# Feature panels of 256 columns with high and low activations in one matmul, in a hybrid decoder layer

## What is computed

```python
proj = x @ w_in[l]                       # 2048 x 13824: q | k | v | rx | ry | gate logits
y_attn = sliding_window_attention(q, k, v, attn_sinks[l]) @ w_attn_proj[l]   # 32 heads of 64, 4 kv heads
rx = causal_dwconv(rx, rnn_conv_w[l], rnn_conv_b[l])                         # 4 taps, 2560 channels
hr = rg_lru(rx, lru_wa[l], lru_ba[l], lru_wi[l], lru_bi[l], lru_lambda[l])
y_rnn = (hr * jax.nn.gelu(ry, approximate=True)) @ w_rnn_proj[l]
g_attn, g_rnn = jnp.split(jax.nn.sigmoid(gl + b_gate[l]), 2, axis=-1)
mix = (g_attn * y_attn + g_rnn * y_rnn) @ w_out[l]
x = layer_norm(ALPHA * x + mix, ln1_g[l], ln1_b[l])
up = x @ ffn_w_up[l]
gate = causal_dwconv(x @ ffn_w_gate[l], ffn_conv_w[l], ffn_conv_b[l])        # 3 taps, 6144 channels
f = (jax.nn.gelu(gate, approximate=True) * up) @ ffn_w_down[l]
x = layer_norm(ALPHA * x + f, ln2_g[l], ln2_b[l])
```

## Time and profile before

| | |
|---|---|
| median of three runs | 1757.09 us |
| the profiled execution | 1758.42 us |
| its span, first to last instruction | 1756.6 us |
| mean granted TensorE clock | 0.991 |
| TensorE, weight loads, VectorE, ScalarE, GpSimd busy | 1717.6, 1636.3, 1033.9, 844.4, 51.1 us |
| moved by DMA | 317.14 MB, mean 181 GB/s |

### The profile page before, as it was taken

One profiled execution on the slowest core, in us unless ns is written; L12 is line 12 of the kernel. 1 busy time (PEld: TensorE's weight loads), 2 busy tenths in 40 slices (PEclk: granted clock), 3 DMA queues, 4 the chain that ended last, 5 costly groups with the idle time before them and its releaser, 6 DMA issues.

```text
span 1756.6 us, 32091 instructions
## 1 busy us (share of the span) xinstructions
PE 1717.6 (98%) x13020; PEld 1636.3 (93%) x13020; DVE 1033.9 (59%) x1182; ACT 844.4 (48%) x1027; POOL 51.1 (3%) x34
## 2 busy tenths in 40 slices
PE   7999999999999999999998999999999999999996
PEld 7999999999999999999877999999889999999885
DVE  5696695444455656556558555556454565656556
ACT  5567566444446656644335444444333444444332
POOL 0000000000000000000003000000000000000002
PEclk9999999999999999999998999999999999999998
DMA  8464453566544343456744555566555555555551
GB/s 295 141 209 158 150 198 128 193 215 199 185 149 168 119 169 131 156 192 218 261 144 144 183 179 187 191 218 200 192 191 186 186 191 190 179 182 190 192 192 72
DMA packets 157141, 317.14 MB, mean 181 GB/s; under 512 B 6008, under 2 KB 11800, under 8 KB 156312
## 3 DMA queue, kind: packets, MB, share of 16 engines
q1 hardware_dynamic: 157080, 316.28, 54.3%
HBM read 314.16 MB, written 2.10 MB: 180 GB/s over the span
## 4 chain that ended last, share of the span: by engine, by line
PE 94%; DVE 4%; ACT 1%; issue 1%; DMA 0%; DVEq 0%; SPq 0%; ACTq 0%
PE bank L268 69%; PE bank L295 20%; PE bank L491 2%; DVE w_lo L246 1%; PE bank L561 1%; PE bank L548 1%; PE bank L280 1%; DVE act_t L1162 1%; ACT s_buf L794 1%; PE bank L539 0%; DVE s_buf L1035 0%; DVE res L1223 0%; DMA x_tok<-in_x_dram 0%; DVE res L1219 0%; DVE smax L1039 0%
## 5 line engine op out<-in xcount | busy, mean ns | idle before, releaser
L268 PE MATMUL bank<-act_t,w_hi 128*128 128x256 f32 x5952 | 1065.6, 281 | 16.0 <-DVE act_t L1162 10.9
L246 DVE TENSOR_TENSOR w_lo<-raw,w_hi 128x1024 fp32r<-128x1024 f32 (+1 forms) x552 | 703.5, 1287 | 619.8 <-ACT w_hi L239 619.7
L239 ACT ACTIVATE w_hi<-raw 128x1024 fp32r<-128x1024 f32 (+1 forms) x552 | 600.2, 1095 | 763.7 <-PE bank L268 559.0
L268 PEld LDWEIGHTS bank<-act_t,w_hi 128*128 128x128 f32 x5952 | 914.3, 189 | 20.8 <-issue 16.6
L268 PE MATMUL bank<-act_t,w_lo 128*128 128x256 f32 x2976 | 834.5, 280 | 0.0
L268 PEld LDWEIGHTS bank<-act_t,w_lo 128*128 128x128 f32 x2976 | 561.3, 189 | 0.0
L295 PE MATMUL bank<-w_hi,f_t 128*128 128x512 f32 x768 | 238.6, 392 | 0.0
L295 PEld LDWEIGHTS bank<-w_hi,f_t 128*128 128x128 f32 x768 | 144.2, 188 | 32.0
L295 PE MATMUL bank<-w_lo,f_t 128*128 128x512 f32 x384 | 150.2, 391 | 0.0
L268 PE MATMUL bank<-g_t,w_hi 128*128 128x256 f32 x640 | 108.9, 276 | 0.0
L268 PEld LDWEIGHTS bank<-g_t,w_hi 128*128 128x128 f32 x640 | 96.6, 188 | 0.0
(11 more groups left out here) (137 smaller groups left out, 960.3 us busy)
## 6 DMA issues: line engine op xcount, KB each, us to landing
raw<-in_w_in_dram SPq DMA_DIRECT2D x52, 1024.0 KB, 5.1
raw<-in_ffn_w_gate_dram SPq DMA_DIRECT2D x48, 1024.0 KB, 5.1
raw<-in_ffn_w_up_dram SPq DMA_DIRECT2D x48, 1024.0 KB, 5.1
raw<-in_ffn_w_down_dram SPq DMA_DIRECT2D x48, 1024.0 KB, 5.1
raw<-in_w_in_dram SPq DMA_DIRECT2D x32, 1280.0 KB, 5.9
raw<-in_w_rnn_proj_dram SPq DMA_DIRECT2D x16, 1280.0 KB, 6.1
raw<-in_w_attn_proj_dram SPq DMA_DIRECT2D x16, 1024.0 KB, 5.2
raw<-in_w_out_dram SPq DMA_DIRECT2D x16, 1024.0 KB, 5.1
```

What stands on the lines that cost most here:

```text
L239: nc.scalar.activation(w_hi[:, slot, 0:size], raw[:, chunk, half:half + size], ACT.Copy)\
L246: nc.vector.tensor_tensor(w_lo[:, slot, 0:size], raw[:, chunk, half:half + size], w_hi[:, slot, 0:size].bitcast(F32), ALU.subtract).then_i ...
L268: last = nc.tensor.matmul(dst, w[:, slot, at_ % size:at_ % size + P], moving[:, kt, part, :], start=(kt == 0 and n == 0 and c % 2 == 0), s ...
```

## The change

- A feature panel has 256 weight columns (two tiles). The accumulator of a tile is a whole bank: w_hi streams high and low activations of a tile of features as one 512 column matmul, w_lo streams the high part, 256 columns, into the first half. The second half is added on the way out: ScalarE copies the first half out of PSUM (`first_half`), VectorE adds the second (`second_half`), and what used to read PSUM (taps, gelu, sigmoid, products) reads the SBUF copy.
- In the recurrence a group has panels of 2, 2 and 1 tiles for rx and the same for ry, 20 units of 1024 columns instead of 16 of 1280. The ry gelu and the product of a group go to the beginning of the next group.
- Chunks have 8 (10) row tiles of 256 columns, in rows of 1 KB, instead of 4 (5) of 512 in rows of 2 KB; the lone tile's chunks have rows of 512 B.
- Recurrence and attention are unrolled; feed-forward loops 12 times per half instead of 6. The attention reads q, k and v where they lie; GpSimd's staging copies go. `s_buf` goes to the ends of `raw`'s slots, the distance table and the transposed probabilities elsewhere.
- After the first LayerNorm, VectorE makes both parts of `act_t`; the affine on `res` goes from GpSimd to VectorE, a piece of 256 columns in each of the first eight turns of `ff0`. TensorE waits for all eight `ln_made` before `ff0`.
- Offsets: `act_t` 82112, `BIG` 118976, `f_t` and `ln_t` +33088, `lru_w_lo` +61760, `lru_w_hi` +75072.

The core of the diff:

```diff
-        act_t = at("act_t", 81920 + 64, [P, KT, 2, T], F32R)
+        act_t = at("act_t", 82112, [P, KT, 2, T], F32R)
-        BIG = SMALL + 3648 + 64
+        BIG = 118976
-        f_t = at("f_t", BIG + 32768, [P, FT_HALF, 2, T], F32R)
+        f_t = at("f_t", BIG + 33088, [P, FT_HALF, 2, T], F32R)
...
-        PASSES = ((w_hi, 0), (w_hi, 1), (w_lo, 0))
+        def panel_features(pe, unit, j0, acc, moving, ks, tiles, units, between=lambda j: None, kt_ready=None):
+            for j in range(units):
+                slot = (j0 + j) % 4
+                pe.wait_ge(lo_made, unit + (j0 + j + 1))
...
+                    nc.tensor.matmul(acc[:, c, :], w_hi[:, slot, at_:at_ + P], moving[:, kt, :, :].rearrange("p h t -> p (h t)"),
+                                     start=(kt == 0), stop=(kt == units * ks - 1), skip_group_check=True)
+                    last = nc.tensor.matmul(acc[:, c, 0:T], w_lo[:, slot, at_:at_ + P], moving[:, kt, 0, :],
+                                            start=False, stop=(kt == units * ks - 1), skip_group_check=True)
...
+            def first_half(name, n, used, dst, tiles=2):
+                wait_apart(unit_used, used)
+                nc.scalar.activation(dst, acc_of(name, n)[:, 0:tiles, 0:T], ACT.Copy).then_inc(half_out, 1)
...
+            def second_half(name, n, dst, tiles=2):
+                dve.wait_ge(half_out, HALVES[name] + n + 1)
+                nc.vector.tensor_tensor(dst, acc_of(name, n)[:, 0:tiles, T:2 * T], dst, ALU.add).then_inc(acc_free, 1)
```

The recurrence on ScalarE, behind the gates of a group (`fill(a, b)` splits units a to b - 1, counted from the group's start):

```diff
+                fill(19, 20)
+                gates(4)
+                fill(20, 21)
+                wait_apart(gates_read, GRP * g + GRP)
+                for c in range(GRP):
+                    nc.scalar.activation(lru_a[:, c, :], lru_r[:, c, :], ACT.Exp, ...
...
+                fill(21, 22)
+                first_half("rxy", panel + 4, unit + 18, g_work[:, GRP * g + 2:GRP * g + 4, 1, :])
+                wait_apart(v_made, g + 1)
+                nc.scalar.activation(group(0), group(0), ACT.Sqrt, scale=2.0 ** 64).then_inc(root_made, 1)
+                fill(22, 24)
```

A block of attention on ScalarE, from its eighth unit on, and the same place on VectorE:

```diff
+                refill(unit, range(11, 12), SLIM)
+                first_half(name, 2 * q + 1, unit + 8, gate[:, 2:4, :])
+                take_o(1)
+                wait_apart(acc_free, PANELS[name] + 2 * q + 4)
+                for c in range(4):
+                    done = nc.scalar.activation(gate[:, c, :], gate[:, c, :], ACT.Sigmoid, bias=param(col + 4 * q + c))
+                done.then_inc(sig_made, 1)
...
+                refill(unit, range(11, 12), SLIM)
+                second_half(name, 2 * q + 1, gate[:, 2:4, :])
+                take_o(1)
+                if name == "gr":
+                    dve.wait_ge(sig_made, q + 1)
+                    part = merge[:, 4 * q:4 * q + 4, :]
+                    nc.vector.tensor_tensor(part, part, gate, ALU.mult).then_inc(merged, 1)
```

A turn of feed-forward on VectorE:

```diff
+                refill(unit, range(6, 8), SLIM)
+                dve.wait_ge(half_out, i * 2 + (HALVES[name] + 1))
+                nc.vector.tensor_tensor(gate_raw[:, :, :], acc_of(name, 0)[:, :, T:2 * T], gate_raw[:, :, :], ALU.add)\
+                    .then_inc(acc_free, 1)
...
+                if affine:
+                    cols = ds(i * 256, 256)
+                    part = res[:, :, cols]
+                    dve.wait_ge(ln_loaded, 32)
+                    dve.wait_ge(ln_turned, 8)
+                    nc.vector.tensor_tensor(part, part, ln_gb[:, 0:1, cols].broadcast_to([P, TOK, 256]), ALU.mult).then_inc(res_made, 1)
```

More of the change, by code:

```diff
@@ L284, in panel_features, with panel_values @@
                 last.then_inc(unit_used, 1)
                 between(j)
+        def panel_values(pe, unit, j0, acc):
+            for j in range(4):
+                slot = (j0 + j) % 4
+                pe.wait_ge(lo_made, unit + (j0 + j + 1))
+                for t in range(TOK):
+                    for k in range(4):
+                        kt = 4 * j + k
+                        for n, (w, part) in enumerate(((w_hi, 0), (w_lo, 0), (w_hi, 1))):
+                            last = nc.tensor.matmul(acc[:, 0, t * T:t * T + T], act_t[:, kt, part, t * P:t * P + P],
+                                                    w[:, slot, k * PW:k * PW + PW], start=(kt == 0 and n == 0 and t == 0),
+                                                    stop=(kt == KT - 1 and n == 2), skip_group_check=True)
+                last.then_inc(unit_used, 1)
@@ L839, in deviation @@
+            unit = UNITS["out"]
+            refill(unit, range(4, 32), SLIM)
             def deviation(t, count):
@@ L877, in _ @@
+                refill(UNITS[f"down{half}"], range(6, 54 if half == 0 else 48), SLIM)
             for t, pieces in enumerate((POOL_PIECES[:2], POOL_PIECES[2:])):
```

1183 lines of the change are left out of this document (610 added, 573 removed).

## The result

The changed kernel takes 1772.57 us (median of 4 runs, 1770.54 to 1772.69), the kernel before 1757.86 beside it (4 runs, 1756.31 to 1761.39). The ratio is 1.0078 with a 95% interval of 1.0061 to 1.0096: slower by 0.8%, where I had forecast 1734 and a range that ended at 1762. Only fast runs are compared in this document; one slow run of the kernel before, in a later series, took 8831.61 us. The profiled execution has a span of 1770.7 us, 14.1 more than before.

The account below looks back on a forecast made before the run. TensorE, busy 98% of the span, was taken as the bound. Terms -34.8 + 1.2 - 2.1 - 1.6 + 11.9 + 10.3 - 7.0 - 0.5 = -22.6 us gave 1734 us, range 1712 to 1762.

Parts of the forecast that it names:

- 1. Pairs: All feature panels: a 512 plus 256 column pair at 341.2 ns; -34.8 us on `act_t`, +1.2 on `g_t` and `o_t`.
- The argument from placement: Matmul operands: address residue modulo 512 sets the pace; moving `act_t` and `BIG` to residue 192 brings 113.0 ns, not 117.6.
- 2. Other operands: Moved operands elsewhere: gates -2.1 us, output projection -1.6, `f_t` in the down projections 0 with bounds -3 and +15.4.
- rival C: Down projections: `f_t` at the residue of w costs the full 15.4 us, total 1749; chance 0.14.
- 3. Two-step eviction: Panel evictions: ScalarE copy plus VectorE add are hidden by TensorE, price 0; without cover 1.3 us per panel.
- 4. Recurrence: Group ends: exp stands behind w_hi of unit 20, stall 3.0 us in each of four groups; +11.9 us.
- 5. Attention: Attention blocks: sigmoids wait for the add, stalls of 1.7 us four times and 1.5 three times; +10.3 us.
- 6. LayerNorm: First LayerNorm: VectorE's slow subtractions go, the wait for all eight `ln_made` is late next; -7.0 us.
- The start: Kernel start: smaller first splits, -0.5 us.
- 7. Transfers: Weight transfers: 1 KB rows at about 65 ns per packet, price 0; the deciding value is 85 ns.
- D: Recurrence and attention: two-step eviction lengthens waits to upper bounds 20 and 16 us, pair at 350 ns; 1778, chance 0.10.
- B: Matmul streams: placement does nothing, a pair costs 350.0 ns, sum +4.1 us, 1761; chance 0.14.

Follow-up runs that it names:

- stream_forms: Layer left out: streams of 24 k tiles after a stop, pairs, reordered pairs, triples and single forms at six distances; at 192 a pair took 353 ns, a triple 340.
- a_triples: Changed kernel with the 512 column w_hi product split into two of 256 columns again, all else kept: 1757.0 us.
- a_all: Changed kernel with triples, unit 20's split later, sigmoids behind the next block's unit 4, and TensorE first waiting for two `ln_made`: 1730.13 us.
- b_act_704: Kernel before with `act_t` alone moved, to offset 85696: 1735.81 us, ratio to before 0.9903.
- a_res0: Changed kernel with `act_t` at 81920 and `BIG` at 118784, a multiple of 512 bytes from w_hi and w_lo: 1770.74 us.
- a_rec: Changed kernel with the split of unit 20 moved behind exponentials and tanhs on ScalarE and behind product v on VectorE: 1762.99 us.
- a_attn2: Changed kernel with only the next block's unit 4 ahead of the attention's sigmoids, unit 5 behind them: 1763.22 us.
- a_ln: Changed kernel with other LayerNorm banks, so TensorE waits for two `ln_made` before the first feed-forward panel, eight before the second: 1766.38 us.
- stream_starts: Layer left out: streams at distances 0 to 192 bytes modulo 512, begun in three ways; triples after a stop at distance 64 took 353 or 340 ns.
- a_all_stop: a_all with two unneeded TensorE waits, ahead of rnn and of the second half of feed-forward: 1730.03 us.
- a_all_stop2: a_all with one unneeded TensorE wait, ahead of the second half of feed-forward: 1728.22 us.

## Why the prediction was wrong

**1. Pairs, -34.8 and +1.2 forecast, 0 and +7.7 measured.** This step failed, and with it the forecast. Both halves of the price were wrong. I took 228.2 ns for a 512 column stream of activations from a row with the activations as weights, where one 512 column product follows another. In the pair it is 235. `stream_forms` shows that a 512 column product has no price of its own (226.7 to 233.3 ns alone, 235 in the pair at distance 192), so a row of another sequence could not give it. And I took 113.0 for its neighbour as a property of the place. It is one of two paces of a stream of 256 column products, and in the pair the neighbour takes 118. `g_t` and `o_t` had the faster pace in the trace of before and lost it: 320 + 256 k tiles at 13.3 ns are 7.7 us, in the table +4.3 and +3.4. With pairs no run shows it at this distance; with triples `g_t` has it again in `a_triples` (108.8 us) but not in `a_all`, and `o_t` in no kernel but before. So that this loss is all the merge's is not shown. My upper bound, 352.8 ns, was right to 0.5 ns, and I had the fitting row (235.2 as twice the 256 column pace) beside the one I chose. With that bound in place of my value the same sum gives 1734.5 + 34.8 = 1769, above the end of my range: the range was narrower than its largest term.
The argument from placement was right in that addresses count for triples: `b_act_704` gained 22 us by moving `act_t`. I applied it to a form that at this distance has no faster pace. By the section of the Trainium skill that the forecast weighed (SBUF — State Buffer, "SBUF: two separate sides"), TensorE waits for no other engine's reads. The streams agree with that: with no other engine at work the paces are still 340 to 360 ns. What differs between them is the distance between the two things that TensorE reads itself, and how the stream begins. The 2.5 ns per matmul of the Trainium skill (TensorE: Matmul & The Clock Gate, "Wait — 56ns, not 53.3ns?") would have saved 8.9 us by merging, an estimate from that figure; the stage ff1, 271.5 in both kernels, shows nothing of it.

**2. Other operands.** Output projection -1.6 forecast, -1.7 measured, but by luck: `a_triples`, with `act_t` where after has it, is back at 89.5 us. Every kernel with pairs has 87.8 here (`a_res0`, with `act_t` elsewhere, 87.0) and every one with triples 89.5, though the stage's own products are the same in all. What ran before it differs. The gates' matmuls went from about 120 to 117 ns, -0.8 for -2.1. `f_t` was forecast at 0 with a bound of +15.4 and gained 1.2 us in each down projection; rival C had the sign wrong. Distance 0 is bad for 256 column products and good for those of 512 (`a_res0` shows it from the other side, 130.5 to 134.3).

**3. Two-step eviction, 0 forecast.** Right: ff1 is 271.5 us in both kernels.

**4. Recurrence, +11.9 forecast, +11.2 measured.** Right in size, and the cause is the one named: exp behind w_hi of unit 20. `a_rec` takes it away and 9.0 us leave the stage, 6.5 at the same clock. That the groups run at 353 and not 341 ns per k tile lowered the wait below the 3.0 us forecast and cost as much in the stream.

**5. Attention, +10.3 forecast, +7.8 measured.** Right in place (seven waits of up to 1.2 us at the scaled values) and somewhat too large, as each unit gave 0.1 us more cover at 353 ns. Only `a_attn2` showed which part of the order counts.

**6. LayerNorm, -7.0 forecast, -9.0 measured.** VectorE's eight subtractions in after, by the groups around the first LayerNorm, take 0.69 us each, where one of before took 5.04:

```profile
L1210 DVE TENSOR_TENSOR act_t<-ln_t,act_t 128x512 fp32r<-128x512 f32 x8 | 5.5, 692 | 0.3
```

I had reckoned one unit, 5.1 us, at 1.2 GHz; 2.9 us of products ran at it, since most of that stretch fell into the wait. The wait for all eight `ln_made` became the next, as said: 5.9 us; `a_ln` takes it away and wins 5.5. The start gave -0.8 for -0.5, but the kernels made from after begin their first product anywhere from 15.5 to 16.8 us, so a gain there is not shown. The 1.1 us more in q and kv I had not listed; 2.1 leave that stage in `a_rec`, so it belongs to the recurrence.

**7. Transfers, 0 forecast.** Right: 0.549 x 16 x 1770.7 us / 284184 packets = 55 ns each, against the 65 of my straight line and the deciding 85. No wait of TensorE goes back to weights in transit. ScalarE's w_hi waited once, at 37 us, 3.8 us for a transfer, which I had named as a sign of being wrong; the chain ran through VectorE's coefficients there.

Without step 1 the terms sum to +11.0 forecast, +6.2 measured. The rival that came nearest was D, longer chains with a pair at 350 ns: 1778. Its stalls were at their upper bounds, and the real ones stood at my own values. B had the pair nearly right (350.0) at a chance of 0.14, but its sum was wrong: at 350.0 ns `g_t` and `o_t` cost 576 x 10.8 = 6.2 us and not 1.2, which makes it 1766, outside my range. What I left without a rival was a stream that loses a pace that it had. The bound for `g_t` and `o_t` ended at +5, where my own 352.8 ns gives +7.8, and it came to +7.7.

## What to carry to other kernels

The pace of a matmul belongs to the sequence in which it stands. Measure a merged product in its own sequence and at its own addresses before pricing 3000 of them from a row of another form; the stream of pairs at distance 192 alone, 353.3 ns, would have turned this forecast. Merging products saved nothing here, where the columns stayed the same. Look first at the distance between moving data and weights modulo 256 bytes, and at the order of long and short products. When an eviction gets a second step, write out each in-order queue from the stall backwards. The splits and sigmoids ahead of a critical exponential cost 19 us here (9.6 and 9.4), and moving them behind it cost nothing that the times show.

## What the hardware showed

- A stream of 256 column fp32r products has two steady paces, 113.3 and 117.8 ns each, at the same addresses, at the full granted clock, and with no other engine at work (`stream_starts`, `stream_forms`, distance 64). It keeps the one with which it began, for as long as 270 us (ff1). Distances 64 and 192 bytes modulo 256 allow the faster; at 0 it is always 120.
- Alternating 512 and 256 columns takes 346.6 to 354 ns per pair, never 340; two by two 345 to 348. Many of the steady periods stand 6.7 ns apart: 340.0, 346.7, 353.3, 360.0.
- A 512 column stream is the other way round: 226.7 at distance 0, 233.3 at 192.
- Behind stops of TensorE of 1.9, 3.9 and 3.9 us the granted clock was at 1.2 GHz for 3.4, 2.9 and 6.2 us of products (`a_all_stop`, `a_all_stop2`). Behind the attention's waits of 1.0 to 1.2 us it stayed at 2.4 GHz.
- Not settled: what in a beginning chooses the pace. The load of the next weights runs beside the products (1471.9 and 1720.2 us busy in a span of 1770.7), and the two reads may fall in or out of step; that fits the dependence on distance, but no run here shows it. One stretch behind a stop had the faster pace and another not.
